# Decoder step with retrieved experts: 192 tokens' experts gathered in place of 160, dense products over 384 columns in place of 416

## The reference, cut to what matters

```
q = (t @ w_q)                         # 8 heads, 2 halves of 128
s = q . sub_keys                      # 128 scores per half
s_top, i_top = top 16 of each half
best_s, best_c = top 16 of the 256 sums   # per head
eid = i1 * 128 + i2                   # 8 x 16 = 128 experts of 16384 per token
g = softmax(best_s)
act = gelu(u_tab[eid] . t)            # u_tab, v_tab: 16384 x 1024
out = sum over the 128 experts of g * act * v_tab[eid]
```

## Time and profile before

| what | value |
|---|---|
| median of 3 runs | 2279.46 us |
| lowest, highest | 2277.97, 2281.86 us |
| span of the profiled execution, its own time | 2278.5 us |
| PE, DVE, POOL, ACT busy | 98%, 70%, 63%, 36% |
| DMA moved | 535.19 MB, mean 235 GB/s |

### The profile page before, as it was taken

The page is one execution under the profiler, slowest core; times in us unless marked ns, Lnnn a source line. Parts: engine busy times, 40 slices in busy tenths (PEclk is TensorE's granted clock), DMA queues, the critical chain, the costliest instruction groups (busy, mean ns, idle before and its releaser), DMA issues.

```text
span 2278.5 us, 38285 instructions
## 1 busy us (share of the span) xinstructions
PE 2236.1 (98%) x14510; PEld 2157.4 (95%) x14510; DVE 1585.6 (70%) x2792; ACT 811.5 (36%) x1194; POOL 1435.2 (63%) x851
## 2 busy tenths in 40 slices
PE   9999999999999999999999999999989999999998
PEld 9999999997799999999999998999989999999998
DVE  7866444546578426237998899999568777777874
ACT  4443223432132002124434334444444444444442
POOL 5554343432354555546878785777778888888873
PEclk9999999999999999999999999999999999999999
DMA  5223222225663232335989886999999999999982
GB/s 215 89 75 140 97 93 97 97 96 184 246 239 128 81 125 79 101 97 197 333 299 311 309 312 229 325 323 340 358 374 390 374 372 372 378 375 376 379 311 79
DMA packets 212800, 535.19 MB, mean 235 GB/s; under 512 B 16816, under 2 KB 101168, under 8 KB 210224
## 3 DMA queue, kind: packets, MB, share of 16 engines
q1 hardware_dynamic: 111392, 234.65, 30.9%
q0 software_dynamic: 46080, 167.79, 19.4%
q10 hardware_dynamic: 55184, 130.77, 15.6%
HBM read 453.89 MB, written 79.25 MB: 234 GB/s over the span
## 4 chain that ended last, share of the span: by engine, by line
PE 72%; DVE 20%; DMA 4%; issue 1%; POOL 1%; ACT 1%; ACTq 0%; DVEq 0%; SPq 0%; POOLq 0%
PE ps L994 36%; PE ps L730 29%; DVE ug L2042 3%; DVE oh_w L2070 2%; DVE oh_a L2066 2%; DVE oh_w L2073 2%; DVE oh_w L2065 2%; DMA cxb<-parked_tiles 1%; DMA gbuf<-gate_scratch 1%; POOL w_lo L704 1%; DVE prev L1841 1%; PE ps L1007 1%; PE ps L907 1%; PE ps L894 1%; PE ps L902 1%
## 5 line engine op out<-in xcount | busy, mean ns | idle before, releaser
L673 POOL TENSOR_SCALAR w_hi<-raw 128x1024 fp32r<-128x1024 f32 x129 | 138.1, 1071 | 518.7 <-issue 388.6
L704 POOL TENSOR_TENSOR w_lo<-raw,e_hi 128x1024 fp32r<-128x1024 f32 x128 | 314.7, 2459 | 124.9 <-PE ps L994 116.7
L704 POOL TENSOR_TENSOR w_lo<-raw,w_hi 128x1024 fp32r<-128x1024 f32 x128 | 316.6, 2473 | 98.6 <-PE ps L994 97.3
L994 PE MATMUL ps<-p_hi,w_lo 128*128 128x416 f32 x1024 | 361.5, 353 | 0.0
L994 PE MATMUL ps<-g_hi,w_lo 128*128 128x416 f32 x1024 | 359.2, 351 | 0.0
L675 POOL TENSOR_TENSOR w_lo<-raw,w_hi 128x1024 fp32r<-128x1024 f32 x129 | 319.8, 2479 | 10.8
L730 PE MATMUL ps<-h_hi,w_hi 128*128 128x288 f32 (+2 forms) x1216 | 274.3, 307 | 1.5 <-ACT ma L1326 1.5
L730 PE MATMUL ps<-h_lo,w_hi 128*128 128x288 f32 (+2 forms) x1216 | 262.9, 298 | 0.0
L730 PE MATMUL ps<-h_hi,w_lo 128*128 128x288 f32 (+2 forms) x1216 | 262.3, 297 | 0.0
L2042 DVE CUSTOM_DVE_ANT_0 ug<-ug,ps 128x1024 f32<-128x1024 f32 x160 | 192.5, 1212 | 56.3 <-DMA ug<-rows_u,eid 45.5
L2051 DVE SCALAR_TENSOR_TENSOR ps<-ug,coef,ps 128x1024 f32<-128x1024 f32 x158 | 203.6, 1289 | 30.4 <-DVE x L2194 25.0
(11 more groups left out here) (357 smaller groups left out, 5093.6 us busy)
## 6 DMA issues: line engine op xcount, KB each, us to landing
raw<-units SPq DMA_DIRECT2D x385, 512.0 KB, 4.7
gate_scratch<-gt SPq DMA_DIRECT2D x52, 512.0 KB, 7.3
activation_scratch<-ge ACTq DMA_DIRECT2D x120, 208.0 KB, 5.4
abuf<-activation_scratch ACTq DMA_DIRECT2D x30, 832.0 KB, 8.8
gbuf<-gate_scratch ACTq DMA_DIRECT2D x30, 832.0 KB, 12.2
prev<-ssm_in ACTq DMA_DIRECT2D x8, 1024.0 KB, 6.5
ssm_s<-prev ACTq DMA_DIRECT2D x8, 1024.0 KB, 4.2
cxb<-parked_tiles ACTq DMA_DIRECT2D x8, 870.0 KB, 6.9
```

Of the source, the lines that this page charges most:

```text
L673: pool.tensor_scalar(w_hi[:, s, :], raw[:, r, :], 1.0, 1.0, ALU.mult, ALU.mult).then_inc(s_whi, 1)
L704: pool.tensor_tensor(w_lo[:, n % 2, :], raw[:, n % RAW, :], e_hi[m % HS_].bitcast(F32), ALU.subtract)\
L994: last = mm(accp[par], w[:, k * P:(k + 1) * P], x_[:, k, t0:t0 + ND], start=k == 0 and i == 0, stop=k == KT - 1 and i == 2)
```

## The change

`SPREAD` goes from 4 to 2. With it `NX` becomes 64 tokens, over two partitions each, `NS` 192, `ND` 384, `NB` 24, and `N_ROW` 192: 64 gathers for spread tokens in place of 32, of each table. `T_HALF` is 384, so `ND > T_HALF` is no longer true: the last half tile's picks are not turned for the gates any more (`N_TURNED` is 3). The dots around the turn of the halves follow from two lists, and one wait counts the stores of the gates in a form that fits 12 pairs of blocks.

```
-SPREAD = 4
+SPREAD = 2
...
-DOTS_U = [9, 0, 0, 1, 1, 1, 1, 1, 1]
-DOTS_V = [2, 2, 2, 2, 2, 2, 3, 2]
+DOTS_U = [18, 2, 2, 2, 2, 2, 2, 2, 2]
+DOTS_V = [4, 4, 4, 4, 4, 4, 3, 3]
...
                     act.wait_ge(s_as[1], 8 * TAIL)
-                    act.wait_ge(s_gs[1], 16 * GQ * (NB // 4 + 1))
+                    act.wait_ge(s_gs[1], 16 * GQ * ((NB // 2 + 1) // 2))
                     act.wait_ge(s_pm, GI // 2)
```

## The result

The changed kernel takes 2304.78 us (median of 4 runs, 2301.4 to 2306.88), the one before, run beside it, 2280.66 (4 runs, 2277.97 to 2283.52): ratio 1.011, 95% interval [1.009, 1.013]. The forecast of 2290.5 had the direction, and the measured time lies in its range, but not in the likeliest case's own range, which ended at 2304. The span of the profiled execution went from 2278.5 to 2304.9 us, +26.4, where the sum said +11.

What follows compares the result with a forecast made beforehand. PE was taken to bound nearly everywhere, with DVE, POOL or DMA 2 to 10% behind. Search -20, gate blocks -13, turn +48, V half 0, end -4 gave +11 on 2278.5, forecast 2290.5 us, range 2262 to 2324.

Steps and rivals of the forecast that it cites:

- the likeliest case: Whole kernel: the forecast itself, 2290.5 us, with its own range 2284 to 2304 and chance 0.43.
- Dense products: All units: 384 columns take 0.1739 us a product, 0.35 us less a unit, 89 us over 256 units if unhindered.
- Search: Units 0 to 78: gathers move forward with PE, DVE waits less for rows; -20 us, bounds 0 and -28.
- Gate blocks: Units 79 to 118: 24 blocks in place of 26, DVE last to arrive; -13 us, bounds -9 and -18.
- Turn: Units 123 to 138: four gathers a unit, POOL's pace, late rows and clock drops; +48 us, bounds +31 and +75.
- the late ring: Turn of the halves: nine slots cover 2.25 units at four rows each, so rows are requested 0.75 units late.
- the falling clock: Turn of the halves: two or three more drops of the granted clock, +5 us.
- the loop behind it: Turn, after V unit 0: low parts, PE and DVE's dots wait on each other; nine units take 66 to 88 us.
- V half: Units 139 to 255: DMA at 400 GB/s keeps 4.54 us a unit; 0 us, bounds -12 and +31.
- rival 3: Whole kernel: search gives the full 28 us, turn +43, V half -3; within 4.6 us of before; chance 0.13.
- Rival 1: V half: DMA sustains less than 400 GB/s, costing up to +31 us, total 2322 us; chance 0.17.
- Rival 2: Turn and V half: ring's delay overlaps, DMA has room; turn +31, V half -12, total 2261 us; chance 0.27.

Runs made afterwards that it cites:

- experiment 1: The changed kernel with 384 columns and 24 gate blocks but only 160 gathers, dots and row sums in each half; -55.2 us against the kernel before.
- experiments 11 and 12: POOL's low parts of units 0 to 78 computed over half their width, in the changed kernel (2282.96 us) and in the kernel before (2269.06 us).
- Experiment 6: The changed kernel with gathers asked for earlier at the turn only, distance falling from 3 units to 1; 2289.01 us.
- experiment 9: The changed kernel with 14 unused products added before each of units 124 to 127 and 129 to 135; 2303.78 us.
- experiment 10: The changed kernel with each load of gates from the second group on cut to one of its twelve blocks; 2289.16 us.
- experiment 2: The changed kernel with 192 gathers and dots at the turn but only 160 gathers and row sums in the V half; u_tab's added rows cost +50.7 us.

## Why the prediction was right in direction and short by more than half

- **Dense products: right.** 0.1745 us a product with 384 columns (forecast 0.174). Without the added rows they take 55 us off the time, 62 in the trace, of the 89 on offer (experiment 1). By the trace the missing part is nearly all in the search and the gate blocks: up to low part 123 they gave 20.0 of 43 us (123 x 0.35), in the turn 3.1 of 5.6, behind it 39 of 41.
- **Search: the step that failed.** -20 was forecast, -8.5 measured, and two premises of the step did not hold. The gathers "move forward with PE, 0.35 us a unit: at most 21 us", near unit 60; but low part 60 came 10.0 us sooner, since PE stood 12.7 us for POOL's low parts, a wait that the working put at nothing, where it had stood 3.5. So DVE's wait for rows fell by 12.6 us and not by 20 (to 16.4, not under 12). And "DVE's search work is the same", but it grew by 5.0 us. Of the 11.5 us missing, 7.4 are thus the wait and 5.0 the work (0.9 came back in other waits). The trace shows single operations that end with POOL's low part; 22 to 31 us of DVE's search and 17.8 of PE's 18.3 idle us vanish with half the low parts' width (experiments 11 and 12). The mechanism stood in the working: its gate-block step set 1.21 us for a one-hot alone against 1.5 to 2.4 on average. It was not carried to the search. Why this kernel's low parts cost DVE 5 us more than the ones before is argued only: they fall on other operations (the copy above, four times in each kernel, took 0.73 us on average for 0.19 before; L2082 went the other way, 1.05 for 1.97), and no run varied their phase alone. Nor did a run ask why POOL hands its low parts to PE later. PE's stand before gate block 0 was forecast over 10 us and is 9.3.
- **Gate blocks: right in mechanism.** -13 forecast, -11.0 by DVE. Its operations gave 15.9, and a wait for PE that the working did not have took 5.0 back. The sign named for it, low parts 79 to 119 some 13 us closer, came out at 6.0. With 0.9 us more up to low part 123, search and blocks together gave 20.3 of 33.
- **Turn: right, 6 us short.** POOL's 7.28 us a unit, the late ring, the wait of DVE for rows and the falling clock are all there. V unit 0 was to end near 55 us after low part 123; the low part that waits for it starts at 55.3. The term mis-sized is the loop behind it: nine units took 84.2 us, near the 88 of a loop without overlap, where 66 to 74 was taken. One sign failed: POOL stood 18.7 us for PE and never over 0.31 for a dot. Experiment 6 prices the lateness at 18 us; 31 of the 54 is POOL's row alone (116.5 - 85.5). The clock was counted as 5 us; with it at 0.87 in place of 0.80 the stage is 5.6 us shorter, but the mean of 0.80 over 139.5 us is deeper than the two or three short drops of the working. The stage of experiment 9 was one execution, and the whole gained 1.0 us.
- **V half: right.** The DMA sustains 400 GB/s with a backlog; 4.54 us a unit forecast, 4.49 measured, and with fewer bytes POOL's 4.42 appeared as the working had it (experiment 10). One sign proves nothing: ACT waited for weights in the kernel before as well. With the end this was -7.3 for a forecast -4.
- **The sum.** 12.7 short in search and blocks, 6 in the turn, 3.3 back behind it: 15.4 of the 15.4 missing.
- **Slips in the working**, none of which moves the forecast: the range says 2262 to 2324 where its rivals' sums are 2261 and 2322; rival 3's terms add up to -5 us, just outside its own 4.6; and "PE is first everywhere" doesn't hold at the turn, where the earlier trace rows has PE at 77.7 of 85.5 and the DMA at 0.99.
- **Rival 1** (less than 400 GB/s) fell: 400 to 405 in four kernels. **Rival 2** fell in both its conditions: over 120 us and more the DMA moved 406 GB/s at most, under 411, and the turn cost over 43. **Rival 3** needed the full 28 us in the search. The edits costed at nothing show no wait of their own after.

## What to carry to other kernels

When an engine that doesn't bound the kernel holds it at one point, ask what of its busy time is its own work: compare an operation's shortest duration with its mean, and look at what its neighbour runs while it is long. And when the bounding engine is made faster, look for the neighbour that hands it its operands: here PE's idle time in the search went from 4.4 to 18.3 us, half of the 28 on offer. Work that is moved from the busiest engine to shared resources should be priced stage by stage with the busiest engine's time already taken away; here the columns' 55 us were real, shrank to 35 beside the added rows, and two stages with 1% to 3% of room took back more than that. A gather's place has a right distance from both sides: too late and the reader waits, too early and the queue that issues it stands in front of other work.

## What the hardware showed beyond the forecast

- A DVE operation of 8 columns, 0.20 us alone, took 2.33 us beside POOL's low part, and ended 0.05 us after it.
- Mixed traffic of one core (weights and activations loaded, rows gathered) holds 400 to 406 GB/s for 120 to 460 us, at a share of 1.02 to 1.03. The share alone doesn't mark the bound: it was 1.02 at 396 GB/s too, where PE was busy for 399.94 of 400 us (experiment 2, 1790 to 2190). The Trainium skill ("DMA: Bandwidth & Descriptors", section "Where 436 GB/s comes from") says that between HBM and SBUF the HBM side of about 358 GB/s binds, a stack's 716 over two cores; the runs here are above it, and below the 435 that the section gives for the fabric.
- The granted clock was 0.50 from 1670 to 1680 us, inside the 40 us of which PE was busy for 20.6. Just before, from 1666.7 to 1674.6, PE had worked in runs of three products with stands of 1.9 and 3.3 us between them. Products in a row start 0.32 us apart there (1675.06 to 1677.30 for seven), where a full stretch has 0.1745.
